# State product ahead of decay arguments and projection, head products behind the projection, in the forward sweep of a state-space stage

## The reference

```python
a_cum = jnp.cumsum(a, axis=2)
seg = a_cum[:, :, :, None] - a_cum[:, :, None, :]
decay = jnp.exp(jnp.where(tri, seg, -jnp.inf))
cb = jnp.einsum('bclgn,bcsgn->bclsg', Cc, Bc)
xdt = xc * dtc[..., None]
y_diag = jnp.einsum('bclsgk,bcsgkp->bclgkp', cb[..., None] * decay, xdt)
decay_out = jnp.exp(a_cum[:, :, -1:] - a_cum)
states = jnp.einsum('bclgn,bclgk,bclgkp->bcgkpn', Bc, decay_out, xdt)
def step(h, inp):
    s, d = inp
    return h * d[..., None, None] + s, h
y_off = jnp.einsum('bclgn,bcgkpn,bclgk->bclgkp', Cc, h_prev, jnp.exp(a_cum))
y = (y_diag + y_off).reshape(b, l, H, P)
```

## Time and profile before

| | us |
|---|---|
| median of 3 runs | 2764.95 |
| lowest, highest | 2759.76, 2764.98 |
| span of the profiled execution | 2760.0 |
| TensorE busy | 2426.7 |
| VectorE busy | 1471.8 |
| ScalarE busy | 1147.1 |
| GpSimd busy | 605.1 |

### The profile page before, as it was taken

One profiled execution on the slowest core, in us unless ns is written; L12 is line 12 of the kernel. 1 busy time (PEld: TensorE's weight loads), 2 busy tenths in 40 slices (PEclk: granted clock), 3 DMA queues, 4 the chain that ended last, 5 costly groups with the idle time before them and its releaser, 6 DMA issues. The chain is left out here.

```text
span 2760.0 us, 36246 instructions
## 1 busy us (share of the span) xinstructions
PE 2426.7 (88%) x12538; PEld 1929.3 (70%) x12538; DVE 1471.8 (53%) x3284; ACT 1147.1 (42%) x2846; POOL 605.1 (22%) x594
## 2 busy tenths in 40 slices
PE   6769989898898989899885999399999999999876
PEld 1338777777777877777664788378878888888555
DVE  1455785859587685858576321613433333333532
ACT  1314545546364645546353111424444444444421
POOL 0011433434243434424241000110110110010000
PEclk8889999999999999999887999599999999999988
DMA  7560001010101001010004431321111211210053
GB/s 259 165 181 31 24 18 52 16 46 16 46 24 39 24 16 54 16 46 16 27 5 160 148 97 54 107 71 31 50 37 53 62 44 33 62 47 16 25 176 98
DMA packets 117261, 172.05 MB, mean 62 GB/s; under 512 B 27576, under 2 KB 78008, under 8 KB 116824
## 3 DMA queue, kind: packets, MB, share of 16 engines
q1 hardware_dynamic: 117080, 169.73, 20.0%
HBM read 141.53 MB, written 30.13 MB: 62 GB/s over the span
## 5 line engine op out<-in xcount | busy, mean ns | idle before, releaser
L599 PE MATMUL sg_pP<-h_h_hi,sg_whi 128*128 128x512 f32 (+1 forms) x1152 | 445.9, 387 | 14.1 <-POOL sg_wlo L1039 14.1
L600 PE MATMUL sg_pP<-h_h_lo,sg_whi 128*128 128x512 f32 (+1 forms) x1152 | 424.7, 369 | 0.0
L601 PE MATMUL sg_pP<-h_h_hi,sg_wlo 128*128 128x512 f32 (+1 forms) x1152 | 424.3, 368 | 0.0
L599 PE MATMUL at_pP<-h_h_hi,at_whi 128*128 128x512 f32 (+1 forms) x640 | 259.0, 405 | 12.0 <-POOL at_wlo L1777 12.0
L599 PEld LDWEIGHTS sg_pP<-h_h_hi,sg_whi 128*128 128x128 f32 x1152 | 232.4, 202 | 47.1 <-POOL sg_wlo L1039 14.2
L600 PEld LDWEIGHTS sg_pP<-h_h_lo,sg_whi 128*128 128x128 f32 x1152 | 231.1, 201 | 32.8
L601 PEld LDWEIGHTS sg_pP<-h_h_hi,sg_wlo 128*128 128x128 f32 x1152 | 229.8, 199 | 34.0
L601 PE MATMUL at_pP<-h_h_hi,at_wlo 128*128 128x512 f32 (+1 forms) x640 | 238.2, 372 | 0.0
L600 PE MATMUL at_pP<-h_h_lo,at_whi 128*128 128x512 f32 (+1 forms) x640 | 237.4, 371 | 0.0
L1777 POOL TENSOR_TENSOR at_wlo<-at_wr,at_whi 128x1024 fp32r<-128x1024 f32 x32 | 75.5, 2358 | 675.0 <-ACT at_whi L1684 675.0
L1737 ACT ACTIVATE at_pm<-at_s,at_nm 128x384 f32<-128x384 f32 x128 | 78.9, 616 | 335.4 <-DVE at_nm L1800 335.4
(11 more groups left out here) (218 smaller groups left out, 5156.2 us busy)
## 6 DMA issues: line engine op xcount, KB each, us to landing
sg_wr<-in_w_ssd SPq DMA_DIRECT2D x48, 512.0 KB, 3.3
at_wr<-in_w_na SPq DMA_DIRECT2D x32, 512.0 KB, 3.8
at_bias<-bt SPq DMA_DIRECT2D x256, 64.0 KB, 2.3
op_yr<-y SPq DMA_DIRECT2D x10, 1024.0 KB, 7.7
md_mod_w<-in_ada_w SPq DMA_DIRECT2D x4, 2048.0 KB, 13.4
nt_mod_w<-in_ada_w SPq DMA_DIRECT2D x4, 2048.0 KB, 10.1
ts_mod_w<-in_ada_w SPq DMA_DIRECT2D x4, 2048.0 KB, 14.2
y<-sg_Z SPq DMA_DIRECT2D x16, 512.0 KB, 3.5
```

The costliest lines, as they stand in the source:

```text
L599: pe.matmul(out, w_hi[:, k, :], h_hi[:, k, t0:t0 + n], start=(k == 0), stop=False)
L600: pe.matmul(out, w_hi[:, k, :], h_lo[:, k, t0:t0 + n], start=False, stop=False)
L601: x = pe.matmul(out, w_lo[:, k, :], h_hi[:, k, t0:t0 + n], start=False, stop=(k == KT - 1))
```

## The change

In each forward step TensorE now issues the off products, then the state product, then the next decay arguments (`forth_state`), then the projection unit, and behind it the head products (`forth_inner`), the sum and the norm's matmuls. The state product thus comes ahead of the arguments, and the head products come behind the projection. The state product's wait for the scan of the step before is covered by the one ahead of the off products; a wait for the end of ScalarE's copies in the backward sweep (`evA`) is now ahead of it too, which in steps after the first has long been met. No other engine's code changes.

```diff
-            def forth(g, c):
+            def forth_state(g, c):
+
                 n = g * NCH + c
                 u0 = ucol(c * P)
-
                 if c:
                     pe.wait_ge(scF, g * (NCH - 1) + c)
...
                 pe.matmul(pO[:, UN:2 * UN], X[:, g % 2, C_, u0:u0 + P], back, start=True,
                           stop=True).then_inc(yoff, 1)
                 if c + 1 < NCH:
+                    pe.wait_ge(evA, (g + 1) * NCH)
+                    pe.wait_ge(xdF, g * (NCH - 1) + c + 1)
+                    pe.matmul(pS[:, 0:UN], X[:, g % 2, B_, u0:u0 + P], xdb[:, :], start=True,
+                              stop=True).then_inc(stF, 1)
                     args(g, c + 1)
 
+            def forth_inner(g, c):
+                n = g * NCH + c
+                u0 = ucol(c * P)
                 pe.wait_ge(mm_, n + 1)
                 pe.wait_ge(evA, (g + 1) * NCH)
                 if n:
...
                 x.then_inc(yd, 1)
-                if c + 1 < NCH:
-                    pe.wait_ge(xdF, g * (NCH - 1) + c + 1)
-                    if c:
-                        pe.wait_ge(scF, g * (NCH - 1) + c)
-                    pe.matmul(pS[:, 0:UN], X[:, g % 2, B_, u0:u0 + P], xdb[:, :], start=True,
-                              stop=True).then_inc(stF, 1)
...
                 for c in range(NCH):
-                    forth(g, c)
+                    forth_state(g, c)
                     if units[g][NCH + c] is not None:
                         unit(units[g][NCH + c])
+                    forth_inner(g, c)
                     off_sum(g, c)
                     norms(g, c)
```

## The result

| us | before | after |
|---|---|---|
| median of the runs | 2764.12 (4 runs) | 2813.11 (4 runs) |
| lowest, highest | 2759.76, 2764.98 | 2809.63, 2816.43 |
| span of the profiled execution | 2760.0 | 2814.5 |
| nine steps of the sweep, summed over groups 0 to 6 | 662.1 | 711.1 |
| the same of group 7 | 67.1 | 74.35 |

After/before is **1.0182**, interval [1.0167, 1.0196]: 1.8% slower, where 2.4% was forecast (2830) and 2801 to 2862 given as the range. The spans differ by 54.5 us: 49.0 in the sweeps of groups 0 to 6, 7.2 in group 7, and the rest of the program is 1.7 shorter. The profiled execution took 2816.27 us, so 1.8 us lie around its span; the 5 us that the prediction added were its distance to a median, and too much.

What follows compares the result with a forecast made beforehand. TensorE, 88% busy, was taken to bound the kernel through its work and standstills. 7 × 7.9 = 55.3 plus 9.6 clock gave +64.9 on 2760.0, 2824.9; with some 5 us around the span, 2830 us (2801 to 2862).

Steps and rivals of the forecast that it cites:

- Which wait takes the place of the one removed: Forward sweep: head products' gate wait goes except in group 7; state product's scaled-input waits grow from 28.5 to 138 us.
- Ordinary steps, +1.2: Steps 2, 3, 5, 6, 8: state product newly stalls 1.2 us (0.9 to 1.6) for its scaled input.
- Step 1, +1.7 and clock +1.6: Step 1: arguments and head products follow the state product, +1.7 us; longer wait drops the clock, +1.6 in 6 groups.
- Pairs 3+4 and 6+7, +1.3 each: Each pair: 1.78 us more TensorE work after the state product, which comes 0.5 earlier; +1.3 us (0.5 to 3.3).
- one long wait for two: Steps 4 and 7: clock loss left unchanged as one wait replaces two; step 4 lost 2.3 us before.
- Rival (a): Pairs 3+4, 6+7: GpSimd's low-weight pass starts before the convolution; pairs cost +3.3 us each, 2858 us total; chance 0.15.
- within 0.2 us of each other: Pairs 3+4, 6+7: estimated gap between the starts of the convolution's second half and GpSimd's low-weight pass.
- (b): Steps 2, 3, 5, 6, 8 of 7 groups: stalls also drop the clock, 1.6 us each; 2886 us; chance 0.07.
- (c): Not slower: clock survives one merged wait in steps 4 and 7, pairs 21.2 us; 2764 or 2758 us; chance 0.08.
- Group 7, 0 (−3 to +5): Last group's forward sweep, without projections: VectorE's queue sets its steps, so later arguments change nothing; 0 us.
- The covers of the projection: Forward steps: a projection (5.7 or 3.1 us) covers the next decays' 2.9 us, so head products don't wait for them.
- The sum: Whole kernel: 55.3 us in seven groups plus 9.6 of clock, +64.9 on the span of 2760.0, giving 2824.9.

Runs made afterwards that it cites:

- e4: Changed kernel with GpSimd scaling the next step's input one step early, ahead of its low-weight pass; 2691.85 us, ratio 0.974 to the kernel before.
- e3: Changed kernel with GpSimd scaling the state product's input before raising the variance to its power, instead of after; 2739.97 us, ratio 0.9928 to the kernel before.
- e8: Changed kernel with throwaway matmuls ahead of the scaled-input wait in groups 0 to 6, 7 in step 1, 10 in steps 4 and 7; 2772.45 us.
- e1: Changed kernel with the state product put back behind the decay arguments, head products still behind the projection; 2762.46 us, ratio 1.0003 to the kernel before.
- e2: Changed kernel with the head products put back ahead of the projection, state product still ahead of the arguments; 2819.73 us, ratio 1.0208 to the kernel before.
- e7: Changed kernel with group 7 alone given the old TensorE order; 2808.14 us, ratio 1.0159 to the kernel before.
- e10: Changed kernel with VectorE's silu moved behind the early part of the norm in forward steps, so the variance comes sooner; 2811.3 us, ratio 1.0172.
- e6: Changed kernel with throwaway matmuls ahead of the scaled-input wait in groups 0 to 6, 12 in step 1, 15 in steps 4 and 7; 2813.19 us.

## Why the prediction was right or wrong

- **Which wait takes the place of the one removed.** Right. The head products' wait for the gate is gone (1.8 us, once), and the state product waits for the scaled input 125.4 us instead of 28.5; forecast 138. e4 takes that wait away and e3 the part of it that stood behind the power (68.5 us are left), and the loss goes with it, with TensorE's order as changed.
- **Ordinary steps, +1.2.** Right for four of the five: +1.16 in steps 5 and 8, +0.93 in 3 and 6 (the lower end named for steps with a silu of 256 tokens). Step 2 has +1.37, where I had argued its larger value of 1.6 away. I had put the step's growth equal to its wait. The waits are 0.95, 0.68 and 1.17 us, so some 0.2 us in each of these steps is growth outside the wait, which I had no term for and no run explains.
- **Step 1, +1.7 and clock +1.6.** +1.37 and +1.65 by e8, together 3.02 for 3.3. The clock did drop, in all groups (and cost 2.9 us in group 5); in group 0, which had the drop already, the step grew by 1.4 alone, from 13.04 to 14.47, as the reading of the earlier trace rows had it. The place in the order cost less, because the state product came 4.43 us after the step's start instead of 4.75: 0.3 us from the earlier start of the weight split, where I had taken 0.1 (wait 3.40, not 3.9).
- **Pairs 3+4 and 6+7, +1.3 each.** This is the step that failed: +0.38 and −0.17. Both trace to two terms. The state product came 13.74 and 13.73 us after the pair's start, instead of 14.53 and 14.27 before: 0.8 and 0.5 earlier, where I took 0.5. The larger error is the sentence "For steps 4 and 7 I leave the loss as it is: one long wait for two". From the state product to the pair's end are 10.46 and 10.11 us after; at full clock it would be 8.86 by the prediction's own terms (9.62 − 2.54 + 1.78), and is 8.74 in e8, where the clock stays at 1.00. So about 1.7 and 1.4 us went to the clock, where before the loss was 2.3 (9.35 − 7.08) and 2.7 (9.76 − 7.08). That is 0.6 and 1.3 us less than I had left in place, some 13 us over seven groups and most of what I forecast too much. Why it is less stays open. It isn't shown that one long wait costs less than two in a row. e1 has one merged wait in step 4 as well, and e2 has the changed kernel's wait in step 7:

```profile
974.54 1.19 PE L832 MATMUL sg_pS<-sg_xdb,sg_X 128*128 128x256 f32 x2 [4.87 <-POOL sg_xdb L1099]
```

```profile
710.38:727.74 17.36, 12.65 (x55) 9.64 (x54) 10.86 (x24) 6.71 (x19) 6.49 (x6) 0.80 0.09 31
```

  In e1, 10.3 us follow that product to the end of the step, against 7.8 in its ordinary steps: 2.5 us to the clock after a single wait. In e2 step 7 takes 17.4 us in two groups and about 15.9 in the others, with the same wait of 4.71 us. And before the change group 0 had step 7 in 15.67 us, with the two waits of the other groups. So such a step lost between 1.4 and 2.8 us to the clock, with one wait as with two. Added up, the clock costs a usual group 4.8 us after the change (1.65 in step 1, 1.7 and 1.4 in steps 4 and 7) and 5.0 before (2.3 and 2.7): what step 1 newly loses, the other two lose less, and the 6.9 us a group are the waits.
- **Rival (a)**, the low-weight pass first. The hold-up happened, but not its price. The timeline of step 4:

```profile
1004.39 2.90 DVE L1146 SCALAR_TENSOR_TENSOR sg_X<-sg_u,sg_par,sg_X 128x513 f32<-128x513 f32 x1
1004.40 2.35 POOL L1041 TENSOR_TENSOR sg_wlo<-sg_wr,sg_whi 128x1024 fp32r<-128x1024 f32 x1 [2.97 <-ACT sg_whi L910]
...
1008.89 0.61 POOL L1099 TENSOR_TENSOR sg_xdb<-sg_X,sg_tab 128x256 f32<-128x256 f32 x1
...
1009.65 1.19 PE L831 MATMUL sg_pS<-sg_xdb,sg_X 128*128 128x256 f32 x2 [4.71 <-POOL sg_xdb L1099]
```

  The convolution's second half (L1146) and the pass (L1041) start 0.01 us apart, and the convolution takes 2.90 us instead of its usual 0.75. It is listed as the first to start and was held up all the same, so at this distance the rows do not follow who started first. But triangles and the first half were ahead of both, so less stood behind it than the +1.5 of the rival assumes. The starts "within 0.2 us of each other" were right, the price of a tie was between my two cases.
- **Rivals (b) and (c)** did not happen: steps 2, 3, 5 have a granted clock of 1.00 with waits of 0.7 to 1.2 us, and steps 4 and 7 have 0.79 and 0.89, so the clock does not survive 4.7 us of waiting. With the waits filled (e8), the pairs are 22.4 us, not the 21.2 of (c).
- **Group 7, 0 (−3 to +5).** Wrong: +7.2, outside its own bounds. I had costed the later arguments at nothing and named VectorE as the cover. That cover is not there:

```profile
1489.04 1.28 ACT L962 ACTIVATE sg_aUh<-sg_le,sg_tab 128x128 fp32r<-128x128 f32 x4 [3.38 <-PE sg_pA L778]
...
1491.39 0.58 ACT L993 ACTIVATE sg_E<-sg_pA 128x512 f32<-128x512 f32 x1
...
1492.00 0.69 DVE L1208 TENSOR_TENSOR sg_E<-sg_E,sg_W 128x512 f32<-128x512 f32 x1 [2.69 <-ACT sg_E L993]
```

  VectorE waits 2.69 us for the exponential here, 10.7 us in six times over the sweep, and not once in that sweep before the change. Gate, variance, power, input, state product, arguments, exponential, masked decays and, behind them in VectorE's queue, the next gate now form one closed loop, and no projection lies in it to run beside. Two runs fit this: e3 and e4 take the input out of the loop, with TensorE's order as changed, and the sweep is 68.5 and 68.2 us. The share of the clock (0.75 over the sweep) isn't separated from it; before the change and in e7 the clock was 0.80 and 0.85 at one and the same length.
- **The covers of the projection.** Right: TensorE is nowhere seen waiting for the masked decays.
- **The sum.** The forecast span was 2824.9 and the measured one is 2814.5. Of the 10.4 us, 15.9 were too many in groups 0 to 6 (64.9 for 49.0), 7.2 were missing in group 7, and 1.7 went elsewhere. The forecast of the time is 17 us too high: these 10.4, then 3 for the surroundings of the span, and 3 by which this profiled execution was above the median.

## What to carry to other kernels

Before a matmul is moved ahead in TensorE's queue, ask which engine makes its operand, and what stands ahead of that operand in that engine's queue. Here an operation of 0.55 us that the operand doesn't need stood ahead of it, with its own wait; putting it behind (e3) or the operand a step earlier (e4) turned a change of +1.8% into −0.7% or −2.6%, more than the order of TensorE's queue is worth in either direction. And a wait has two prices, its length and the clock behind it. Read both from the windows of a step, over several groups, since the second came out at 0 to 2.9 us for one and the same wait.

## What the runs showed of the hardware that I had not expected

- A wait of 3.3 to 4.7 us usually cost 1.4 to 1.9 us more in clock (but nothing in two groups of e10, and 2.8 to 2.9 in single groups of the changed kernel and e2). Matmuls whose result is thrown away buy that back (e8: −41 us), as long as they end before the operand comes. One of these products, 256 columns and two matmul records in the trace, took 0.43 to 0.45 us (4.48 us for ten), and 12 and 15 of them overran it by as much as they gained (e6).
- The same wait of 1.95 us in the backward sweep leaves the clock at 1.00 in one run and drops it to 0.78 in another, with the same queue around it. Why isn't settled; it is worth 1.5 us a group, and makes differences under 9 us between two of these kernels uncertain as to their cause.
- A GpSimd operation of 128 x 1 took 0.93 us instead of 0.55 beside a VectorE operation of 128 x 512 that had started first, and a convolution pass took 2.90 us instead of 0.75 beside the low-weight pass that started 0.01 us after it.
